# Block-diagonal powers and inverses of an RWKV chunk: transposes by VectorE in place of TensorE products

## The reference, cut to what matters

```python
def rwkv7_recurrence(r, w, k, v, a, b):
    def step(s, inp):
        r_t, w_t, k_t, v_t, a_t, b_t = inp
        sa = jnp.einsum('bhvk,bhk->bhv', s, a_t)
        s = s * w_t[:, :, None, :] + sa[..., None] * b_t[:, :, None, :] + v_t[..., None] * k_t[:, :, None, :]
        return s, jnp.einsum('bhvk,bhk->bhv', s, r_t)
...
h = modulate(rms_norm(x, norm_g[l, 1]), sh1, sc1)
x = x + (1 + gt1)[:, None, :] * token_mixer(
...
```

## Time and profile before

| | us |
|---|---|
| median of 3 runs | 1531.95 (1531.02 to 1535.5) |
| the profiled execution, its own time | 1532.11 |
| span of the profiled execution | 1530.4 |
| TensorE busy | 1488.9 (97%) |
| VectorE busy | 904.8 (59%) |
| ScalarE busy | 262.6 (17%) |
| GpSimd busy | 76.3 (5%) |

### The profile page before, as it was taken

How to read it: one execution, slowest core, us unless ns; L and a number is a source line. 1 busy time by engine, 2 the same in 40 slices (tenths; PEclk the granted TensorE clock), 3 DMA queues, 4 the chain that set the end, 5 groups by cost and what they waited for, 6 DMA issues and landing times.

```text
span 1530.4 us, 27256 instructions
## 1 busy us (share of the span) xinstructions
PE 1488.9 (97%) x11846; PEld 1355.8 (89%) x11846; DVE 904.8 (59%) x1770; ACT 262.6 (17%) x523; POOL 76.3 (5%) x143
## 2 busy tenths in 40 slices
PE   5999999999999998999999999999999999999998
PEld 4899999788888888999989999988888888899998
DVE  5588877554434326888866768665633432655454
ACT  2100002532222020000030000035222200200001
POOL 7001000000000000000000000000000000000000
PEclk7999999999999999999999999999999999999999
DMA  9789997243321575889866878743341247466550
GB/s 333 229 281 307 304 306 221 84 124 97 86 56 57 173 241 162 272 280 288 271 196 216 267 243 271 205 125 124 110 110 30 57 156 243 124 187 189 176 165 28
DMA packets 306231, 282.91 MB, mean 185 GB/s; under 512 B 15368, under 2 KB 269696, under 8 KB 306112
## 3 DMA queue, kind: packets, MB, share of 16 engines
q1 hardware_dynamic: 287168, 211.12, 46.0%
q0 software_dynamic: 17952, 69.21, 13.2%
q10 hardware_dynamic: 992, 0.85, 0.2%
HBM read 280.10 MB, written 1.05 MB: 184 GB/s over the span
## 4 chain that ended last, share of the span: by engine, by line
PE 95%; DVE 2%; DMA 1%; ACT 1%; issue 0%; ACTq 0%; SPq 0%; DVEq 0%
PE ps L1376 94%; DMA arena<-in_ada_w_dram 1%; PE ps L1380 1%; DVE ada_acc L852 1%; ACTq L642 0%; ACT rs L567 0%; DVE y_both L1247 0%; ACT hT L567 0%; DVE hT L883 0%; ACT arena L567 0%; DVE hT L886 0%; SPq L434 0%; DVE arena L1286 0%; DVE ada_turn L858 0%; DVE arena L1281 0%
## 5 line engine op out<-in xcount | busy, mean ns | idle before, releaser
L1376 PE MATMUL ps<-hT,ring 128*128 128x256 f32 (+2 forms) x2768 | 500.2, 336 | 4.8 <-ACT hT L567 4.8
L1376 PEld LDWEIGHTS ps<-hT,ring 128*128 128x128 f32 (+1 forms) x2768 | 436.6, 191 | 61.7 <-issue 10.7
L1376 PE MATMUL ps<-arena,ring 128*128 128x256 f32 (+1 forms) x1568 | 355.5, 381 | 4.4 <-DVE arena L928 4.4
L1376 PEld LDWEIGHTS ps<-arena,ring 128*128 128x128 f32 x1568 | 293.0, 191 | 42.0 <-DVE arena L928 4.8
L1376 PE MATMUL ps<-y_both,arena 128*128 128x128 f32 x1848 | 219.9, 275 | 0.0
L1376 PEld LDWEIGHTS ps<-y_both,arena 128*128 128x128 f32 x1848 | 212.8, 192 | 0.2
L852 DVE SCALAR_TENSOR_TENSOR ada_acc<-ada_stage,cond,ada_acc 128x512 f32<-128x512 f32 x231 | 173.5, 751 | 9.0 <-DMA ada_stage<-in_ada_w_dram 1.1
L1376 PE MATMUL ps<-y_both,ring 128*128 128x128 f32 (+1 forms) x872 | 137.3, 306 | 0.0
L937 DVE TENSOR_TENSOR arena<-arena,ps 128x256 f32<-128x256 f32 x77 | 32.3, 420 | 176.0 <-ACT arena L603 175.9
L1376 PEld LDWEIGHTS ps<-y_both,ring 128*128 128x128 f32 x872 | 123.3, 191 | 6.4
L603 ACT ACTIVATE arena<-ps 128x128 f32<-128x128 f32 x77 | 21.3, 277 | 580.6 <-PE ps L1376 580.6
(11 more groups left out here) (228 smaller groups left out, 1064.6 us busy)
## 6 DMA issues: line engine op xcount, KB each, us to landing
ring<-in_ffn_w_in_dram SPq DMA_DIRECT2D x176, 512.0 KB, 5.3
ada_stage<-in_ada_w_dram POOLq DMA_DIRECT2D x66, 1024.0 KB, 7.2
ring<-in_ffn_w_out_dram SPq DMA_DIRECT2D x88, 512.0 KB, 6.5
ring<-in_mix_w_in_dram SPq DMA_DIRECT2D x46, 512.0 KB, 5.1
ring<-in_mix_w_in_dram SPq DMA_DIRECT2D x12, 1024.0 KB, 5.4
ring<-in_mix_w_in_dram SPq DMA_DIRECT2D x6, 1536.0 KB, 6.4
ring<-in_mix_w_out_dram SPq DMA_DIRECT2D x8, 1024.0 KB, 5.2
arena<-in_ada_w_dram SPq DMA_DIRECT2D x6, 1024.0 KB, 17.9
```

The lines of the kernel that those rows point to most:

```text
L1376: return nc.tensor.matmul(out_, lhsT, rhs, start=start, stop=stop, **kw)
```

## The change

Each transposed copy is made by VectorE from the copy in SBUF. VectorE's transposition turns every 32x32 block in place; the matrices concerned have nonzero elements only in their diagonal 16x16 or 32x32 blocks, so turning each 32x32 block is the whole transposition.

- TensorE no longer issues `p2t`, `p4t`, `x32` and `x64`: 4 pairs of batches per stage.
- ScalarE evacuates `p2`, `p4`, `g32` and `g64`, which VectorE did, in place of the four that are gone. Its number of copies stays at 10 a stage.
- VectorE makes `p2t` and `p4t` once ScalarE has copied `p2` and `p4`, and `x32` and `x64` from `xt` right behind the growths "xt 8" and "xt 32". A transposition of one half stands between the growths of the two halves.
- `p4t` gets room of its own instead of the place of `nt`. The wait for the copy "turned b" moves from the batch `p2t` to ahead of z0.

```diff
-        p2, p2t, xt = (carve(8, 64) for n in range(3))
+        p2, p2t, p4t, xt = (carve(8, 64) for n in range(4))
...
-                    copy("p2t", p2t, 1)
-                    copy("p4t", m_t[:, :, 0, :], 1)
+                    copy("p2", p2, 0)
+                    copy("p4", m_n[:, 0], 0)
...
-                    copy("x32", p2t, 0)
+                    copy("g32", p2, 1)
...
-                    copy("x64", p2t, 0)
+                    copy("g64", p2, 1)
...
-                    def evac(label, n, dst, bank):
-                        dv.wait_ge(*PE.at(l, f"{label} {g} {n}"))
-                        free(V.tensor_copy(dst[:, 4 * n:4 * n + 4, :], half(n, bank)), f"{label} {g} {n}")
+                    def flipped(label, n, dst, source):
+
+                        a, b = (t[:, 4 * n:4 * n + 4, :].rearrange("p i n -> p (i n)") for t in (dst, source))
+                        free(V.transpose(a, b), f"{label} {g} {n}")
...
-                        evac("p2", n, p2, 0)
+                        dv.wait_ge(*AC.at(l, f"p2 {g} {n}"))
+                        flipped("p2t", n, p2t, p2)
...
-                        evac("p4", n, m_n[:, 0], 0)
+                        dv.wait_ge(*AC.at(l, f"p4 {g} {n}"))
+                        flipped("p4t", n, p4t, m_n[:, 0])
                         grow("xt 2", n)
...
-                    for label in ("xt 4", "xt 8"):
+                    for n in range(2):
+                        grow("xt 4", n)
+                    for size, label in ((32, "xt 8"), (64, "xt 32")):
                         for n in range(2):
                             grow(label, n)
-                    for size in (32, 64):
-                        for n in range(2):
-                            evac(f"g{size}", n, p2, 1)
-                        for n in range(2):
-                            grow(f"xt {size}", n)
+                            dv.wait_ge(*DV.last(l))
+                            flipped(f"x{size}", n, p2t, xt)
+                    for n in range(2):
+                        grow("xt 64", n)
...
-                        batch("p2t", n, 1, n16, nt, [AC.at(l, f"turned b {g}")])
...
-                        batch("p4", n, 0, p2t, p2, [DV.at(l, f"p2 {g} {n}"), AC.at(l, f"p2t {g} {n}")])
+                        batch("p4", n, 0, p2t, p2, [AC.at(l, f"p2 {g} {n}"), DV.at(l, f"p2t {g} {n}")])
...
-                        batch("p4t", n, 1, p2, p2t, [])
...
-                        batch("p8", n, 0, nt, n16, [DV.at(l, f"p4 {g} {n}"), AC.at(l, f"p4t {g} {n}")])
+                        batch("p8", n, 0, p4t, n16, [AC.at(l, f"p4 {g} {n}"), DV.at(l, f"p4t {g} {n}")])
                         batch("xt 4", n, 2, n16, xt, [DV.at(l, f"xt 2 {g} {n}")])
+                    pe.wait_ge(*AC.at(l, f"turned b {g}"))
...
-                            batch(f"x{size}", n, 0, xt, None, [DV.at(l, f"{before} {g} {n}")])
-                            batch(f"g{size}", n, 1, off, xt, [AC.at(l, f"z0 {g}")])
+                            batch(f"g{size}", n, 1, off, xt, [DV.at(l, f"{before} {g} {n}"), AC.at(l, f"z0 {g}")])
...
-                            batch(f"xt {size}", n, 2, p2t, p2, [AC.at(l, f"x{size} {g} {n}"),
-                                                                DV.at(l, f"g{size} {g} {n}")])
+                            batch(f"xt {size}", n, 2, p2t, p2, [DV.at(l, f"x{size} {g} {n}"),
+                                                                AC.at(l, f"g{size} {g} {n}")])
```

More of the change, by code:

```diff
@@ L1790, in batch @@
                                 dst = ps[c, 3 * n + bank, at:at + wide]
-                                last = mm(dst, lhsT[c, i, :], ident2[c, :] if rhs is None else rhs[c, i, :])
+                                last = mm(dst, lhsT[c, i, :], rhs[c, i, :])
                         last.then_inc(*PE.step(f"{label} {g} {n}"))
```

## The result

Beside the kernel before on one chip, the changed kernel took a median of 1523.75 us (seven runs, 1519.76 to 1526.81) against 1531.95 us (seven runs, 1530.47 to 1537.62). The ratio of all executions is 0.9933, 95% interval 0.9914 to 0.9953: 10.3 us faster (7.2 to 13.2) than 1532, while the two medians alone lie 8.2 us apart. One execution of the kernel before, beside e1 to e4, took 3129.53 us, twice the usual, and is left out everywhere. The forecast was 1522.0 in a range of 1518 to 1526, and the saving it summed was 9.98 us. In a later comparison, with six runs of the same kernel, the ratio was 0.9933 again.

What follows compares the result with a forecast made beforehand. TensorE, busy 97% of the span, was taken to bound the kernel. Stage gains of 2.56 us (first groups) and 2.43 (second), over two layers 9.98, took 1532.11 us to 1522.1, median 1522.0, range 1518 to 1526.

Steps and rivals of the forecast that it cites:

- The gross gain: Transposing products removed from TensorE: 8 batches a stage at 0.467 us, 3.74 us a stage, 14.9 us in four stages.
- The transposition: VectorE's transposition of 128x256, a size not yet seen: 0.445 us, between bounds of 0.42 and 0.71.
- rival (a): Transposition (0.71 us) dearer: 1524.1 us; with another 0.1 us on four hand-overs a stage, 1525.7 us; chance 0.10.
- The first half: Each stage from the start of p2 0 through the first gate columns: 3.68 us against 4.81, 1.13 us gained.
- The second half: Each stage from g32 0 to gate columns "c": 3.88 us; gained 1.43 us in first groups, 1.30 in second groups.
- The sum: Four stages: 2.56 us a first group, 2.43 a second group, two layers, 9.98 us of 14.9 gross.
- The head sums: VectorE, second groups: growth xt 4 some 0.5 us late behind them, about 0.7 us to spare, covered by z0; priced nothing.
- (b): Rival: new waits no longer than those they replace, so nearly the whole gross gain, 14.9 us: 1517.1 us; chance 0.04.
- (c): Rival: waits of 0.2 to 0.7 us in the stages let TensorE's clock fall to 1.2 GHz: 1547.6 us; chance 0.02.
- (d): Rival: unseen TensorE issue gap, say 0.3 us at each of four new waits a stage, 4.8 us: 1526.8; chance 0.08.
- (e): Rival: no change or a little slower, the same gaps costing 0.6 us each, 9.6 us: 1531.6 us; chance 0.03.

Runs made afterwards that it cites:

- e1: The changed kernel with x32 and x64 as TensorE products again, only p2t and p4t transposed by VectorE; 1526.07 us, ratio 0.9953.
- e4: The changed kernel with a spare transposition of the same size, never read, ahead of each real one; 1529.33 us, ratio 0.9963.
- e5_growths_first: The changed kernel with both halves of xt 32 grown before x64 is transposed; 1519.82 us, ratio 0.9912.
- e2: The changed kernel with p2t and p4t as TensorE products again, only x32 and x64 transposed by VectorE; 1525.82 us, ratio 0.9946.
- e3_no_transposition: The changed kernel with all transpositions left out and their targets zeroed once a group; 1519.71 us, ratio 0.9913.
- e6: The changed kernel with two gate products moved between p2 and p4 in every stage; 1520.91 us, ratio 0.9925.
- e7: The changed kernel with the edits of e5_growths_first and e6 together; 1520.66 us, ratio 0.9917.
- e9: The kernel of e7 run once more, unedited; 1520.93 us, ratio 0.9920.
- e11: The kernel of e7 with two gate products moved from the tail to far ahead of the stage, so the weight load is issued earlier; 1518.20 us, ratio 0.9897.

## Why the prediction was right, point by point

**The gross gain** held as far as it can be told: 512 matmuls are gone, and batches still follow each other at 0.467 us. The 15.3 us less of busy time, close to 14.9 as it is, is no proof of it (above).

**The transposition** was put at 0.445 us between bounds of 0.42 and 0.71. All 32 took 445 to 447 ns. The step that subtracts, from the transposition of 128x512, what halving saves a copy, gives 0.457 (0.712 less 0.255); the 0.445 that was then taken is more than a rounding, and that it is exact to the nanosecond is luck. The part of rival (a) on the transposition falls with it; of its dearer hand-overs a smaller piece is real (0.05 and 0.08 us, below).

**The first half** was to take 3.68 us and took 3.75. The timeline shows each step, beside the start at 411.32:

```profile
412.05 0.85 ACT L567 ACTIVATE arena<-ps 128x256 f32<-128x256 f32 x2
412.47 0.91 DVE L1282 STREAM_TRANSPOSE arena<-arena 128x256 f32<-128x256 f32 x2 [4.04 <-ACT arena L567]
413.03 1.97 PEld L1380 LDWEIGHTS ps<-arena 64*64 64x64 f32 x64 [0.70 <-ACT arena L567]
413.06 2.08 PE L1380 MATMUL ps<-arena 64*64 64x64 f32 x64 [0.59 <-DVE arena L1282]
```

The copy starts at 0.73 and the transposition at 1.15 (forecast 0.73 and 1.14). The first transposition ends at 1.60 and the weights of p4 0 load at 1.71, not 1.65: the hand-over from a transposition to TensorE is 0.11 us, not the 0.06 read in the earlier trace rows behind a growth. That is the mis-sized term, 0.06 us a stage. The wait stands as 0.70 on the weight loads, against 0.72.

**The second half** was to take 3.88 us and took 3.85 and 3.84. Its steps, from 421.07 on:

```profile
422.30 1.04 PEld L1380 LDWEIGHTS ps<-arena 64*64 64x64 f32 x32 [0.22 <-issue]
423.05 0.42 DVE L1287 TENSOR_TENSOR arena<-arena,ps 128x256 f32<-128x256 f32 x1 [1.70 <-PE ps L1380]
423.50 0.45 DVE L1282 STREAM_TRANSPOSE arena<-arena 128x256 f32<-128x256 f32 x1
423.52 0.54 PEld L1380 LDWEIGHTS ps<-arena 64*64 64x64 f32 x16 [0.19 <-DVE arena L1287]
423.87 0.38 DVE L1287 TENSOR_TENSOR arena<-arena,ps 128x256 f32<-128x256 f32 x1
...
424.31 0.54 PEld L1380 LDWEIGHTS ps<-arena 64*64 64x64 f32 x16 [0.24 <-DVE arena L1287]
```

xt 32 0 begins at 1.23 (forecast 1.15): ScalarE's copies run from 0.73 to 1.11, so the hand-over from ScalarE to TensorE was 0.12 and not the estimated 0.04. g64 0 begins at 2.45 (2.36). Then the second growth starts at 2.80, 0.37 behind the transposition's start rather than 0.45, and g64 1 is at 3.24 (3.26). Two errors of 0.08 us cancelled, and the length came out right by luck in that part. e5_growths_first removed the wait ahead of g64 1 and got 0.32 us for it, not 0.43.

**The sum** was 9.98 us, measured 9.70. 0.28 us of difference is the first half, 1.06 gained a stage in place of 1.13. The second halves came to the forecast sum, but by two differences that cancel: 1.46 us in the first group of layer 0 and 1.34 in both second groups, where 1.43 and 1.30 were forecast, and 1.33 in the first group of layer 1, where 1.43 was. That group was taken as equal to that of layer 0, but its stretch was 5.18 us before and not 5.31 (the stage 17.05 and not 17.18), so it had less to give.

**The head sums** of the second groups were to make the growth xt 4 0 about 0.5 us late with 0.7 to spare. Of the second group's VectorE rows, the end of the sums and the growth:

```profile
457.15 0.74 DVE L1038 TENSOR_REDUCE stat<-arena 128x4 f32<-128x256 f32 x2
457.81 0.41 DVE L1287 TENSOR_TENSOR arena<-arena,ps 128x256 f32<-128x256 f32 x1
```

The growth starts at once behind them, which is late by about 0.25 us and not 0.5 (the wait of the earlier trace rows is gone), and xt 8 0 starts at 459.16, 0.9 us behind the growth's end. The cover held; the second groups gained 2.39 and 2.39 us, and e1 and e2 show the two halves of it: 1.06 and 1.33.

**The rivals.** (b), nearly the whole gross gain, fails by the 0.85 us of idle time a stage, and e3_no_transposition and e4_doubled show two transpositions a stage on TensorE's path. (c), the clock: 1.00 in all four stages, and in those of all twelve experiments. By the rule of the Trainium skill, "TensorE: Matmul & The Clock Gate", section "A second HAM failure mode: psum-queue depth-cycling", that short idle moments between groups of matmuls can make the clock swing, it should have shown in the stages with four waits of 0.2 to 0.7 us; there the traces disagree with it, at 1.00. (d) and (e), an unseen issue gap behind each new wait: none beyond the hand-overs of 0.11 and 0.12 us. But an issue gap does exist, up to three times the 0.6 us of (e) at a single place: it came in e6, e7 and e9, from an edit worth 0.6 us a stage that looked free. The prediction called it a wait that it does not see; it stayed away from this change, whose order of gate products is the old one.

**The range.** The median of 1523.75 lies 1.75 us above 1522.0. 0.28 us of that is the sum; the rest is within what the comparison can tell (the interval of the saving is 7.2 to 13.2 us).

## What to carry to other kernels

Where one engine bounds the kernel and its stream is a chain of small products, moving a step to an idle engine pays the product's time less what the new serial hand-overs cost. Here 65% of it stayed (9.7 of 14.9 us), and the sum was foreseen within 3% by writing down for each half of a stage who starts when; where the halves of a tile run behind each other, two of the eight transpositions of a stage stand on the path, one for each half of the stage. After the move, look at what the new engine does first: a transposition stood ahead of a growth that TensorE waited for, and swapping them gave another 1.3 us in the stages. When bulk products are moved to fill a wait, follow the buffers that they release, since the load that these trigger can cost more than the wait.

## What was not expected of the hardware

**Instructions can arrive late behind a bulk load.** TensorE stood for 0.4 to 1.9 us with no semaphore in its way, at the same product in e6, e7 and e9 (0.58, 1.59 and 1.87 us) and four matmuls earlier in e11 (0.37), when a block of instructions of 0.02 MB came 4.5 us or more behind the stage's start, while 1 MB of weights was being loaded. In all four the hole lies behind 8204 matmuls of the program, and TensorE came back 2.5 to 2.7 us after the block's packet had started. Moving the load removed it. That the late block is what TensorE stood for is argued, from these two constants.

**A VectorE instruction that has nothing to wait for starts before the one ahead has ended**: 0.32 to 0.37 us behind the start of a transposition of 0.40 to 0.45 (e4_doubled, and the growth behind a transposition in the changed kernel).

**The whole time goes with the mean granted clock of the execution, not with the kernel alone.** Of 25 executions of the kernel before, beside e1 to e4, those at a mean clock of 0.991 had spans of 1527.2 to 1527.7 us, at 0.988 of 1530.1 and 1532.6, and at 0.983 of 1535.9 to 1536.2; a straight line through all has 1.2 us for 0.001 of clock, with a correlation of −0.93. The loss lies outside the stages and at changing places. The same stretch of one kernel, in e7_both and then e9_both_again:

```profile
1080.00:1120.00 40.00, 40.00 (x218) 35.60 (x217) 18.38 (x44) 10.52 (x14) 0.00 (x0) 1.00 0.31 92
```

```profile
1080.00:1120.00 40.00, 40.00 (x187) 34.87 (x186) 22.38 (x49) 7.87 (x10) 0.00 (x0) 0.91 0.32 92
```

TensorE was busy throughout in both, and did 218 matmuls in one and 187 in the other. What lets the clock fall there was not tried. It is why a change of 1 us can be read from the windows of these traces, but not from the time of the kernel.
